# Two transformer blocks on one core: the general path of the expert layers out of line, loads issued behind a block end, and more down-projection pieces kept outside the ring

## What is computed

```python
def expert_block(args):
    xb, cb = args
    gate = jnp.einsum('td,edf->tef', xb, w_gate)
    up = jnp.einsum('td,edf->tef', xb, w_up)
    act = jax.nn.silu(gate) * up * cb[..., None].astype(xb.dtype)
    return jnp.einsum('tef,efd->td', act, w_down)
```

## Time and profile before

| | |
|---|---|
| median of 3 runs | 1620.88 us (1620.79 to 1625.31) |
| profiled execution | 1610.42 us, its span 1608.7 us |
| mean granted TensorE clock | 0.977 |
| PE busy | 1455.6 us (90%) |
| DVE, ACT, POOL busy | 758.8, 493.4, 100.4 us |
| read from HBM | 462.81 MB, 289 GB/s over the span |
| MoE pair loops (first L1564 to the last L1602) | 203.9 to 422.7, 621.0 to 840.1, 1213.4 to 1318.2, 1496.7 to 1601.4 us |

### The profile page before, as it was taken

One profiled execution on the slowest core, in us unless ns is written; L12 is line 12 of the kernel. 1 busy time (PEld: TensorE's weight loads), 2 busy tenths in 40 slices (PEclk: granted clock), 3 DMA queues, 4 the chain that ended last, 5 costly groups with the idle time before them and its releaser, 6 DMA issues. The chain is left out here.

```text
span 1608.7 us, 23934 instructions
## 1 busy us (share of the span) xinstructions
PE 1455.6 (90%) x9314; PEld 808.9 (50%) x9314; DVE 758.8 (47%) x1621; ACT 493.4 (31%) x987; POOL 100.4 (6%) x242
## 2 busy tenths in 40 slices
PE   7999999888799899998779998998999969999996
PEld 4586533222375554322227876787663327756332
DVE  1656432222434635222226655764674337587433
ACT  3222211111215402111125655665312126651211
POOL 0000011100000001110101001000001101000110
PEclk9999999999999999999999999998999999999999
DMA  9985589999862186999997551435187994518796
GB/s 366 372 342 215 230 338 421 420 421 421 367 262 112 53 361 260 421 420 421 421 423 282 199 203 40 157 132 192 38 366 303 420 423 170 233 46 331 327 420 272
DMA packets 62399, 467.31 MB, mean 290 GB/s; under 512 B 7696, under 2 KB 15808, under 8 KB 17472
## 3 DMA queue, kind: packets, MB, share of 16 engines
q1 hardware_dynamic: 62272, 465.59, 71.5%
HBM read 462.81 MB, written 2.76 MB: 289 GB/s over the span
## 5 line engine op out<-in xcount | busy, mean ns | idle before, releaser
L1564 PE MATMUL PS<-ring,catT 128*32 128x512 f32 x3072 | 347.4, 594 | 36.2 <-issue 27.6
L793 PE MATMUL PS<-w_split,h_split 128*128 128x512 f32 x1152 | 271.6, 395 | 6.6 <-DVE w_split L878 6.6
L793 PEld LDWEIGHTS PS<-w_split,h_split 128*128 128x128 f32 x1152 | 214.6, 189 | 57.0 <-DVE w_split L878 8.4
L1564 PEld LDWEIGHTS PS<-ring,catT 128*32 128x32 f32 x3072 | 99.6, 109 | 253.1 <-issue 253.0
L1587 PE MATMUL PS<-ring,hidden_cols 128*32 128x512 f32 x1472 | 167.0, 593 | 32.2 <-issue 26.8
L878 DVE TENSOR_TENSOR w_split<-ring,w_split 128x512 fp32r<-128x512 f32 x192 | 133.3, 709 | 68.1 <-ACT w_split L826 67.6
L826 ACT CAST w_split<-ring 128x512 fp32r<-128x512 f32 x192 | 118.0, 619 | 105.7 <-PE PS L793 105.1
L1713 ACT ACTIVATE hidden_rows<-PS 128x256 f32<-128x256 f32 x48 | 18.4, 384 | 393.4 <-PE PS L1564 393.4
L1587 PEld LDWEIGHTS PS<-ring,hidden_cols 128*32 128x32 f32 x1472 | 50.2, 109 | 143.0 <-issue 143.0
L413 DVE SCALAR_TENSOR_TENSOR ada_part<-ring,silu_c,ada_part 128x768 f32<-128x768 f32 x98 | 99.8, 1019 | 3.4
L484 PE MATMUL PS<-ring,catT 128*128 128x512 f32 x224 | 99.1, 602 | 1.0 <-PEq L986 1.0
(11 more groups left out here) (410 smaller groups left out, 1745.5 us busy)
## 6 DMA issues: line engine op xcount, KB each, us to landing
ring<-in_moe SPq DMA_DIRECT2D x284, 1024.0 KB, 18.5
ring<-in_w_ada SPq DMA_DIRECT2D x16, 3072.0 KB, 12.4
ring<-in_a_w_in SPq DMA_DIRECT2D x23, 2048.0 KB, 12.6
ring<-in_b_w_in SPq DMA_DIRECT2D x8, 2048.0 KB, 22.7
ring<-in_a_w_out SPq DMA_DIRECT2D x2, 3072.0 KB, 11.4
ring<-in_b_w_out SPq DMA_DIRECT2D x2, 3072.0 KB, 9.8
ring<-in_w_mem_kv SPq DMA_DIRECT2D x2, 2048.0 KB, 12.3
first_down<-in_moe SPq DMA_DIRECT2D x4, 1024.0 KB, 11.3
```

Source lines behind the costliest of these rows:

```text
L793: last = nc.tensor.matmul(PS[:, 2 * (i % 2) + t, :], hs[:, hp, k, t * P:(t + 1) * P], wk[:, (KT * i + k) % splits, wp, :], start=k == 0 an ...
L1564: last = nc.tensor.matmul(PS[lanes, 4 + i % 2, :].rearrange("p (g f) -> p g f", g=2), xf[:, i % 2, k, lanes], gate_up_weights(2 * i + q % ...
```

## The change

1. The number of down pieces outside the ring goes from (2, 2, 0, 0) to (3, 4, 2, 2). `first_down` holds two in every layer; the third lies in `hT`, the fourth (layer 1 only) in one tile, `mem_kv`, that now holds `mkT` and `mv`. The third's load waits for `router_ready` and is issued last of them.
2. In `project_rows` ahead of a router, SP issues only chunks with `need` up to the index of the last weight chunk, `place[-1]`. The rest is issued by the MoE stage's own first `stream.issue`.
3. The general path's code of all four layers is placed behind the last layer's code of each engine; the fast path branches to the next block instead of going past an `Else`. As `hT` may hold a down piece, the general path turns `x` again into `h_again`. The fast path gets one more semaphore increment on PE (`xt_ready`) and on DVE (`xt_taken`).

```diff
-FIRST_DOWN = 2
+ASIDE = (3, 4, 2, 2)
...
-        c_moe0 = experts("moe0", 32, FIRST_DOWN)
+        c_moe0 = experts("moe0", 32, ASIDE[0])
-        c_moe1 = experts("moe1", 32, FIRST_DOWN)
+        c_moe1 = experts("moe1", 32, ASIDE[1])
-        c_moe2 = experts("moe2", 16)
+        c_moe2 = experts("moe2", 16, ASIDE[2])
-        c_moe3 = experts("moe3", 16)
+        c_moe3 = experts("moe3", 16, ASIDE[3])
...
-        mkT = sbuf(first_block, "mkT", [P, 4, T])
-        mv = sbuf(first_block, "mv", [P, TT, 512])
+        mem_kv = sbuf(first_block, "mem_kv", [P, PIECE])
+        mkT = mem_kv[:, 0:4 * T].rearrange("p (h t) -> p h t", h=4)
+        mv = mem_kv[:, 4 * T:PIECE].rearrange("p (t d) -> p t d", t=TT)
...
-                    stream.issue(nc, sp, first + len(widths) + n_ada)
+                    stream.issue(nc, sp, place[-1] if router is not None else first + len(widths) + n_ada)
...
+        def far_from_here(name, at, back, program):
+
+            dense_programs[name].append((at, back, nc.cur_bb, [(s, s.base) for s in names.values()], program))
+
+        def place_dense_programs(name, eng):
+
+            for n, (at, back, ahead_of_branch, bases, program) in enumerate(dense_programs[name]):
+                nc.switch_bb(at, parent=ahead_of_branch)
...
+                program(eng)
...
+                if n + 1 < len(dense_programs[name]) or back[0] == "r":
+                    ENGINES[name].br(back)
...
-                aside = FIRST_DOWN if m < 2 else 0
-                first_down = sbuf(st, "first_down", [P, aside, PIECE]) if aside else None
+                aside = ASIDE[m]
+                first_down = sbuf(st, "first_down", [P, 2, PIECE])
+                aside_at = [first_down[:, 0, :], first_down[:, 1, :], hT[:].rearrange("p k t -> p (k t)"), mem_kv[:]][0:aside]
+                h_again = spare[:, 2 * T:2 * T + KT * T].rearrange("p (k t) -> p k t", k=KT)
...
-                    for e in range(aside):
-                        nc.sync.dma_start(first_down[:, e, :], A[f"moe{m}"][e][:, 2 * PIECE:3 * PIECE]).then_inc(down_loaded.sem, 16)
+                    for e in sorted(range(aside), key=lambda e: e == 2):
+                        if e == 2:
+                            sp.wait_ge(*r_ready.at(1))
+                        nc.sync.dma_start(aside_at[e], A[f"moe{m}"][e][:, 2 * PIECE:3 * PIECE]).then_inc(down_loaded.sem, 16)
...
-                    with nc.tensor.If(fits(nc.tensor) > 0):
+                    far_from_here("tensor", f"many_{m}", block.end_bb, every_token)
+                    nc.tensor.br_cond(fits(nc.tensor) > 0, on_true=f"few_{m}", on_false=f"many_{m}")
+                    nc.switch_bb(f"few_{m}")
...
+                    nc.tensor.sem_inc(xt_ready.sem, 4)
+                    if then == "store":
+                        nc.tensor.br(block.end_bb)
+                        place_dense_programs("tensor", pe)
...
-                                if c == 1 and 2 * i >= aside:
-                                    nc.scalar.sem_inc(chunk_used, 2)
+                            if c == 1 and 2 * i + 1 >= aside:
+                                nc.scalar.sem_inc(chunk_used, 2 if 2 * i >= aside else 1)
...
-                    with nc.vector.If(fits(nc.vector) > 0):
+                    far_from_here("vector", f"every_product_{m}", f"rejoin_dve_{m}", every_token)
+                    before_branch = nc.cur_bb
+                    nc.vector.br_cond(fits(nc.vector) > 0, on_true=f"product_{m}", on_false=f"every_product_{m}")
+                    nc.switch_bb(f"product_{m}", parent=before_branch)
...
+                    nc.vector.sem_inc(xt_taken.sem, 4)
+                    nc.vector.br(f"rejoin_dve_{m}")
+                    nc.switch_bb(f"rejoin_dve_{m}", parent=before_branch)
```

More of the change, by code:

```diff
@@ L1391, in down_weights @@
                 def down_weights(e):
-                    w = first_down[:, e, :] if e < aside else stream.raw(piece(e, 2))
+                    w = aside_at[e] if e < aside else stream.raw(piece(e, 2))
                     return w.rearrange("p (k f) -> p k f", k=2)
@@ L1439, in _, with every_token @@
                     pool.wait_ge(*table_ready.at(1))
[L1440 to L1452, removed]
-                        for j in range(4):
-                            nc.gpsimd.sem_inc(cb_loaded[j].sem, 16 * (E // 4))
-                        nc.gpsimd.sem_inc(c_stored.sem, 16)
-                    with nc.gpsimd.Else():
+                    def every_token(pool):
                         pool.wait_ge(*ct_sb.at(1))
@@ L1609, in _, with every_token @@
                     pe.wait_ge(*table_ready.at(1))
[L1610 to L1631 removed]
+                    def every_token(pe):
                         pe.wait_ge(*xs_taken_act.at(KT // 2))
@@ L1735, in _ @@
                         nc.scalar.activation(stat[:, 2, 0:TT], stat[:, 1, 0:TT], ACT.Sqrt).then_inc(rt_ready.sem, 1)
+                    if then == "store":
+                        nc.scalar.br(block.end_bb)
+                        place_dense_programs("scalar", act)
                 @block.vector
@@ L1912, in _, with every_token @@
-                    with nc.vector.Else():
+                    def every_token(dve):
                         dve.wait_ge(*weight_made.at(1))
@@ new lines, in _ @@
+                    slots(0)
+                    for i in range(NP):
+                        if i:
+                            gate_rows(i - 1, 0)
+                        hidden(i)
+                        if i:
+                            gate_rows(i - 1, 1)
+                            low(i - 1, 0)
+                        if i and i + 1 < NP:
+                            low(i - 1, 1)
+                        take_turned(i)
+                        if i + 1 == NP:
+                            low(i - 1, 1)
+                        else:
+                            slots(i + 1)
@@ new lines, in _ @@
+                    gate_rows(NP - 1, 0)
+                    low(NP - 1, 0)
+                    gate_rows(NP - 1, 1)
+                    low(NP - 1, 1)
+                    if gate is not None:
+                        nc.vector.sem_inc(rows_gated.sem, TT)
+                    nc.vector.sem_inc(hid_ready.sem, E - NP)
+                    nc.vector.sem_inc(c_ready.sem, 1)
+                    nc.vector.sem_inc(comb_parts.sem, 2)
+                    nc.vector.sem_inc(up_taken.sem, E)
+                    nc.vector.sem_inc(h_scaled.sem, KT)
@@ L1965, in _ @@
                             nc.vector.tensor_scalar(x_normed[:, t, :], x[:, t, :], rs[:, t:t + 1], None, ALU.mult)
+                    if then == "store":
+                        nc.vector.br(block.end_bb)
+                        place_dense_programs("vector", dve)
                 for s in (gate_ready, up_ready, silu_ready, hid_ready, up_taken, dense_down):
```

240 lines of the change are left out of this document (129 added, 111 removed).

## The result

The changed kernel takes 1597.8 us (median of 4 runs, 1594.5 to 1598.3); the kernel before took 1620.8 us in runs beside it (4 runs, 1614.7 to 1625.3). The ratio is 0.986, with a 95% interval of 0.982 to 0.989: 1.4% faster, and at the forecast 1597.8. The profiled execution takes 1594.5 us, its span is 1592.7. That is 16.0 us less span than before, not the 23.1 of the sum. So the median came out right and the profile didn't, and the parts have to be looked at one by one.

A forecast was written before the change was run, and what follows sets the result against it. The prediction took memory to bound the pair loops, idle ahead of them. Pieces with later issues (21.1 us) plus code out of line (2.0) gave 23.1 us, off the median 1620.9: 1597.8 us, range 1587 to 1607.

The forecast's parts named there:

- What bounds the kernel: Pair loops wait for memory, idle ahead of them; each piece loaded then outside the ring saves 2.49 us.
- Rival 4: Added loads are hidden anyway or merely moved, so memory ends when it did: gain 0 to 5 us, chance 0.05.
- Rival 2: Ends give nothing and layer 2's fill overruns, eating part of the earlier start: gain 15.5 to 20.5 us, chance 0.24.
- Rival 3: Memory runs slower in the timed runs, so pieces are worth more: gain 26 to 30 us, chance 0.06.
- Pieces aside: Down pieces loaded outside the ring: one more in layer 0 (2.5 us), two more in each other layer (5.0 each).
- it fits, 2 x 2.49 = 5.0 us: Layer 1: the fill ends at 618.1, before loop loads at 625.8, so two added pieces save 5.0 us.
- Layers 2 and 3: 5.0 each: Two pieces outside the ring in each of these layers shorten its loop by 5.0 us.
- The pieces can return no more than the waits there are: 5.1: Layer 2: the loop's 5.1 us of waits cap the gain, so two pieces' 5.0 us just fits.
- Later issues: SP's loads moved behind the block's end: 1.3 us ahead of layer 2, 2.3 ahead of layer 3, nothing in layer 1.
- Out of line: General path moved away from MoE stage ends: between 4.6 us gained and 1.4 lost, taken as 2.0 gained.
- Rival 5: Fast-path entries and returns wait for instructions: at 4 us each the kernel is 11 us slower, 1632; chance 0.05.
- 10.5 us above it; I take the difference off that: Median 1620.9 exceeds the profiled 1610.4 by 10.5 us; the gain was subtracted from the median, giving 1597.8.

The follow-up runs named there:

- earlier issue: The changed kernel with edit 2 undone, so loads are issued ahead of the block's end again: 1595.3 us.
- PE in line: The changed kernel with PE's general path back between the fast path and what follows; DVE, ACT and POOL stay out of line: 1601.6 us.
- PE in line in layer 0 alone: The changed kernel with PE's general path back in its old place in layer 0 only: 1597.5 us.
- repetition: The changed kernel run and profiled once more with no edit: 1594.0 us, ratio to the kernel before 0.983.
- DVE and ACT in line: The changed kernel with DVE's and ACT's general paths back in their old place, PE's and POOL's still behind the last layer: 1598.4 us.
- fastest kernel: The changed kernel with three pieces aside in layers 2 and 3, and loads issued at the old place ahead of layer 1: 1589.5 us, ratio to the kernel before 0.984.

## Why the prediction came out as it did

**What bounds the kernel: right.** The loops of layers 0 and 1 run at memory's pace before and after, and a piece outside the ring is worth one piece's time: 2.4 us for one in layer 0, 25.4 us for eleven. Rival 4 (transfers hidden anyway) is refuted: memory works in what was quiet, and the waits fall with it, by 2.1 us in layer 0, where the loop falls by 2.4. Rival 2 is refuted too, though its 15.5 to 20.5 us would hold the 16.0 of the profiles: the ends gave 3.7 us, and no fill ran into its loop (3.0 and 4.6 us of quiet are left). Rival 3 (slower memory in the timed runs) finds no support: from 660 to 760 us, inside layer 1's loop, memory gives 421 GB/s in the profile of before (1610.4 us) and in one of 1620.6 us, that of the later issue alone.

**Pieces aside: mechanism right, layer 1 mis-sized.** The step "it fits, 2 x 2.49 = 5.0 us" gave 2.6. It did fit: memory is quiet from 618.2 to 625.9, and the forecast said from 618.1. What failed is the assumption behind it, that once the loop's loads run, they run at one pace to the end. In this arrangement one load lands 2.4 us late, and all after it are as late. Edits that take one condition away (earlier issue 214.0, PE in line 213.8, PE in line in layer 0 alone 213.9) get the 5 us. How the place of PE's instructions delays a load of weights isn't shown. PE goes on fetching instructions while the loop runs. This is the view of the queues in the changed kernel, 621 to 838 us:

```profile
q1 hardware_dynamic: 11837, 88.64, 98.5%
q8 instruction: 14, 0.23, 0.4%
q14 instruction: 6, 0.05, 0.1%
```

These 20 packets share the DMA engines with loads that leave no slack, and both an edit that moves the fetches and one that moves the loads make the late load go. The number of packets is the same in the run with PE in line in layer 0 alone (14 and 6), which hasn't the loss, but their times differ. In the four loops with the loss a q8 packet starts 43.2 to 44.4 us after the loop does, and the load that lands 44.5 to 45.1 us into the other five loops with four pieces aside lands at 46.2 to 47.3. Of those five, two have that packet at 42.9 and 43.0, and three have none between 37 and 48 us. That fits a packet that comes in the way of one load, and doesn't show it: the packet is 16 KB, a 64th of the load, and the trace doesn't say which of the 16 engines was late. The lower clock isn't the cause: this loop has it only from 802 to 807 us (0.66), long after the late load, and the run with the earlier issue has it from 760 to 765 us (0.69) in a loop of 214.0. So the cause stays open.

**Layers 2 and 3: 5.0 each was right, and the profiled run had less.** The changed kernel's profile has 3.8 and 3.3, its repetition 5.0 and 4.9. Layer 2's loads had a slow start: the loop's first load takes 7.1 us from issue to landing where it takes 6.3 in the repetition, from the sixth on each lands 1.2 us behind the repetition's, and 2.1 us of waits are left against 1.1. Why it was slow isn't shown. Layer 3's first pair ran partly at 1.2 GHz (0.66 in 1485 to 1490), which shows in L1597: 59.4 us busy where layer 2's loop beside it has 57.7. The other runs confirm this price. With two pieces aside, layer 3's loop is 101.4 to 101.7 us in the four profiles with 59.4 (changed kernel, pieces aside alone, PE in line, three aside in layer 1) and 99.6 to 99.8 in the four with 57.7 (repetition, earlier issue, DVE and ACT in line, PE in line in layer 0). "The pieces can return no more than the waits there are: 5.1" was too low: with three pieces aside 6.3 us went from layer 2's loop. The idle time of its two groups fell by 5.3 of this, from 9.1 us (4.8 in the earlier trace rows, and 4.3 over the whole loop of before, below) to 3.8:

```profile
L1587 PE MATMUL PS<-ring,hidden_cols 128*32 128x512 f32 x256 | 29.0, 593 | 4.3 <-issue 2.5 <-DVE hidden_cols L1852 1.6
```

The last 1.0 us stands in no group's idle time, so the view of groups can't give such a limit to the microsecond.

**Later issues: right beside the kernel before, worth nothing in the whole.** The gaps fell by 1.3 and 2.3 as worked out, and the fill took as long as said (26.5 us in both layers). But the two edits share layer 3's 2.3 us: 1.0 comes from the two loads fewer that the pieces aside leave in front of the block's end. "In layer 1 the later issue is worth nothing" was the wrong sign: there it costs one piece's time together with the other two edits. Taking the edit back leaves the time where it was (1595.3 against 1597.8 and 1594.0 in the two sets of runs of the changed kernel). Keeping it ahead of layers 2 and 3 alone is what the fastest kernel does.

**Out of line: the cause right, the term too low.** I took 2.0 us between 4.6 and -1.4; it is 3.7 in the profile for the three exits, 4.1 by medians with this edit alone. The reason I gave for the low value, increments that stay, was wrong, since DVE's 0.35 us is gone too. The sum that I bounded it by was also put together wrongly: 3 x 1.06 and DVE's 0.35 lie side by side in part, as the two runs with one engine in line show (6.56 and 5.95 against 5.47). Rival 5 is refuted: entries and returns of the fast path cost nothing that shows; from layer 1's first turn of `x` to its loop it is 21.9 us before and after. Each exit of a general path in line moves an instruction packet, and none moves without it, in the same kernel too. The Trainium skill (Runtime: NRT & Kernel Launch, Instruction fetch mechanics) says that a taken branch out of the two pages held waits for a DMA fetch of its target; by this rule the trace agrees, with 1.1 to 1.5 us on PE here.

**The frame: two errors that cancelled.** Profile to profile the sum was 7.1 us too large: the loops 5.4 short, the ends 1.7 over, and 3.3 us lost elsewhere. That loss goes with the clock: the granted clock is 0.971 where it was 0.977. The stages between layer 0's exit and layer 1's MoE stage, whose work the change leaves as it was, take 169.5 us at 0.98 before and 172.8 at 0.96 after; other stretches lose and gain smaller amounts. The stretches before the loops come out in steps, layer 2's from its first turn of `x` to the loop 23.1 us before, 24.7 after, and 26.3 in two other runs. In 1190 to 1195 PE runs at 0.50, the level of 1.2 GHz, after five microseconds without a pause (5.00 busy in 1185 to 1190, 0.84). I had put nothing for this. On the other side, "10.5 us above it; I take the difference off that" assumed that the runs of both kernels stand as far from their profile. The profiled execution of before was among its fastest (1607.5 to 1625.3 us over all but one stray run), with one of the highest clocks (0.977, of 0.966 to 0.979); that of the changed kernel is only 3.3 us below its median. This gave back 7.2 us. So the mean forecast was right by its largest terms and by luck in the last 7 us.

## What to carry to other kernels

Where a loop waits for memory and memory is idle ahead of it, each piece loaded outside the ring is worth its transfer time, until the waits are gone. Work out how many pieces fit, and measure with one more than that. Here code that is never run but stands between two stages costs at every stage end, side by side on the engines, so that the engine that comes last sets the price. Two edits that each pay alone can share one gain or undo it: run the whole with each part taken back, not only each part alone.

## What was not expected of the hardware

A load of 1 MB among 80 equal ones in a loop landed 2.4 us late at the same place in two executions of one kernel (1.3 and 2.2 us late in two variants of it), and was on time when 1,500 never executed matmuls of another layer were put elsewhere in PE's program. The lower clock comes in lumps of about 1.65 us lost each (23.1, 24.7, 26.3 us for the same stretch). In the middle of a memory-bound loop a lump cost nothing: in layer 0 of the fastest kernel L1597 is busy for 117.6 us in place of 115.9, and the loop is 216.5 us as without it. In the loop's first pair it delays the first free ring place, and with it every load behind: 1.6 to 2.0 us in layer 3.
